# Start of the expert stages of a two-layer decoder trunk: expert 0's rows copied by halves, its gate and up products in PSUM banks 2 and 3, expert 1's first unit and the one-hot turning placed earlier

## The reference, cut to what matters

```python
for i in range(2):                                   # two layers, 512 tokens, 1024 wide
    m = short_conv_mixer(x) if i == 0 else chunked_sgu_mixer(x)
    x = layer_norm(ALPHA * x + m, ln_mix_g[i], ln_mix_b[i])
    # grouped_moe: 16 experts in 4 groups, the best group and two experts in it per token
    scores = sigmoid(x @ router_w); gates = normalised scores of the two chosen
    for e in range(16):
        h = silu(x @ w_gate[e]) * (x @ w_up[e])      # 1024 -> 512
        f = f + gates[:, e] * (h @ w_down[e])        # 512 -> 1024
    x = layer_norm(ALPHA * x + f, ln_ffn_g[i], ln_ffn_b[i])
```

## Time and profile before

| | |
|---|---|
| median of 3 runs | 1126.11 us (1125.99 to 1126.21) |
| profiled execution, its own time | 1129.59 us |
| span of the profiled execution | 1127.8 us |
| PE busy | 1104.9 us (98%) |
| DVE busy | 830.3 us (74%) |
| ACT busy | 652.2 us (58%) |
| POOL busy | 119.1 us (11%) |
| DMA moved | 295.97 MB, mean 262 GB/s |

### The profile page before, as it was taken

How to read it: one execution, slowest core, us unless ns; L and a number is a source line. 1 busy time by engine, 2 the same in 40 slices (tenths; PEclk the granted TensorE clock), 3 DMA queues, 4 the chain that set the end, 5 groups by cost and what they waited for, 6 DMA issues and landing times.

```text
span 1127.8 us, 15394 instructions
## 1 busy us (share of the span) xinstructions
PE 1104.9 (98%) x5448; PEld 871.9 (77%) x5448; DVE 830.3 (74%) x1022; ACT 652.2 (58%) x761; POOL 119.1 (11%) x104
## 2 busy tenths in 40 slices
PE   8999999899999999999999999999999999999996
PEld 7888888577777777778888888888757777777774
DVE  4553547899988999999516555535799798988996
ACT  4322323588887888853417332213558788887872
POOL 2000000031111111030000000000004111111013
PEclk9999999999999999999999999999999999999998
DMA  8925421699999999987304222440399999999986
GB/s 309 418 82 221 149 94 40 227 403 391 393 380 393 371 393 378 399 273 273 149 19 174 88 76 77 156 141 38 121 352 369 395 375 391 377 385 384 383 290 171
DMA packets 51752, 295.97 MB, mean 262 GB/s; under 512 B 8932, under 2 KB 9092, under 8 KB 22128
## 3 DMA queue, kind: packets, MB, share of 16 engines
q1 hardware_dynamic: 36096, 252.46, 58.0%
q0 software_dynamic: 9040, 20.91, 6.4%
q10 hardware_dynamic: 6560, 21.87, 5.1%
HBM read 277.07 MB, written 29.62 MB: 272 GB/s over the span
## 4 chain that ended last, share of the span: by engine, by line
PE 82%; DMA 10%; DVE 3%; issue 2%; ACT 1%; ACTq 0%; SPq 0%; POOL 0%; DVEq 0%; POOLq 0%
PE ps L481 24%; PE ps L483 24%; PE ps L482 24%; DMA raw_more<-in_w_moe 4%; PE ps L2046 2%; DMA raw<-in_w_dense 2%; PE ps L1963 2%; DMA X<-y_rows 1%; PE ps L1888 1%; DVE lo L477 1%; PE ps L2186 1%; PE ps L1870 1%; DMA raw<-in_w_moe 1%; PE ps L1859 1%; PE ps L1988 1%
## 5 line engine op out<-in xcount | busy, mean ns | idle before, releaser
L477 DVE TENSOR_TENSOR lo<-raw,hi 128x1024 fp32r<-128x1024 f32 x320 | 376.5, 1219 | 89.0 <-ACT hi L466 86.5
L466 ACT ACTIVATE hi<-raw 128x1024 fp32r<-128x1024 f32 x320 | 325.0, 1056 | 120.8 <-PE ps L483 80.2
L481 PE MATMUL ps<-hi,xgT_hi 128*112 128x512 f32 x480 | 190.7, 397 | 0.0
L483 PE MATMUL ps<-hi,xgT_lo 128*112 128x512 f32 x480 | 188.6, 393 | 0.0
L482 PE MATMUL ps<-lo,xgT_hi 128*112 128x512 f32 x480 | 187.9, 391 | 0.0
L477 DVE TENSOR_TENSOR lo<-raw_more,hi 128x1024 fp32r<-128x1024 f32 x128 | 153.3, 1220 | 32.9 <-ACT hi L466 30.5
L466 ACT ACTIVATE hi<-raw_more 128x1024 fp32r<-128x1024 f32 x128 | 132.8, 1057 | 56.1 <-DMA raw_more<-in_w_moe 37.1
L481 PE MATMUL ps<-xT_hi,hi 128*128 128x512 f32 x320 | 126.5, 395 | 1.4 <-DVE lo L477 1.4
L482 PE MATMUL ps<-xT_lo,hi 128*128 128x512 f32 x320 | 124.7, 390 | 0.0
L483 PE MATMUL ps<-xT_hi,lo 128*128 128x512 f32 x320 | 124.6, 389 | 0.0
L483 PEld LDWEIGHTS ps<-hi,xgT_lo 128*112 128x112 f32 x480 | 83.7, 174 | 26.5
(11 more groups left out here) (216 smaller groups left out, 1490.0 us busy)
## 6 DMA issues: line engine op xcount, KB each, us to landing
raw<-in_w_moe SPq DMA_DIRECT2D x128, 1024.0 KB, 12.7
raw_more<-in_w_moe SPq DMA_DIRECT2D x64, 1024.0 KB
raw<-in_w_dense SPq DMA_DIRECT2D x39, 1024.0 KB, 5.6
y_rows<-X ACTq DMA_DIRECT2D x4, 2048.0 KB, 25.3
X<-y_rows POOLq DMA_DIRECT2D x10, 512.0 KB, 9.2
x_rows<-X ACTq DMA_DIRECT2D x8, 512.0 KB, 2.6
Y<-y_rows SPq DMA_DIRECT2D x6, 512.0 KB, 5.5
xT_raw<-in_x_t SPq DMA_DIRECT2D x4, 512.0 KB, 6.5
```

The lines of the kernel that those rows point to most:

```text
L466: nc.scalar.activation(hi[:, s, :], flat(raw_units(n)), ACT.Copy).then_inc(hi_ready, 1)
L477: eng.tensor_tensor(lo[:, s, :], flat(raw_units(n)), hi[:, s, :], ALU.subtract).then_inc(lo_ready, 1)
L481: nc.tensor.matmul(out_, a_hi, b_hi, start=first, stop=False)
L483: return nc.tensor.matmul(out_, a_lo, b_hi, start=False, stop=last)
```

## The change

The copies of expert 0's rows are signalled by halves. A new semaphore is raised by product 3 of the last tile, the last that writes bank 5, and ACT's copy waits for it in place of the end of the tile. ACT then waits for the end of the tile before it scales the token tiles, behind a table load. `gate_up_first` starts on ACT's half alone and waits for DVE's half before its product 4.

Expert 0's gate and up go to banks 2 and 3, so that `gate_up(1)` in banks 0 and 1 has no need to wait for `hidden(0)`. Its unit 0 stands directly behind `gate_up_first`, and `turn_h(0)` behind unit 0. `turned_hot` is placed behind unit 6 instead of behind the whole of `gate_up(1)`. On ACT the copy to `hotT` is placed before the `hi` of unit 12 instead of behind `silu(1)`.

The counts move to bank 7, the ids of layer 1 from bank 3 to bank 7. The wait for `most_ready` goes from `turned_hot` to the first `gates_to_slots`, and DVE's `route_most` goes from behind the `lo` of unit 7 to between `x_lo(1)` and `hidden(0)`.

```diff
-        IDA = (7, 3)
+        IDA = 7
+        CNT = 7
@@ ACT, silu
-                    nc.scalar.activation(sgate[0:T, :], ps[0:T, 0, :], ACT.Silu).then_inc(silu_ready, 1)
+                    bank = 2 if is_zero(c) else 0
+                    nc.scalar.activation(sgate[0:T, :], ps[0:T, bank, :], ACT.Silu).then_inc(silu_ready, 1)
@@ ACT, turn(e)
                     for k in range(GU - 1):
+                        if is_zero(e) and k == DN:
+                            act.wait_ge(hotT_in, layer + 1)
+                            copy(hotT[layer][0:T, :, :], ps[0:T, 2:4, :]).then_inc(hotT_ready, 1)
                         if n0 + k not in WHOLE:
                             split_hi(act, n0 + k, step, i)
                     silu(e + 1, step, i)
-                    if is_zero(e):
-                        act.wait_ge(hotT_in, layer + 1)
-                        copy(hotT[layer][0:T, :, :], ps[0:T, 2:4, :]).then_inc(hotT_ready, 1)
@@ ACT, start of the experts
-                act.wait_ge(xgT_ready, m0 + 1)
+                act.wait_ge(x0_half, layer + 1)
                 copy(x0[:, 0:4, 0:T], slots(ps[:, 5:6, :])).then_inc(xgT_hi_ready, 1)
                 preload(ACT.Silu)
+                act.wait_ge(xgT_ready, m0 + 1)
@@ DVE, hidden
-                    nc.vector.tensor_tensor(hid[0:T, :], sgate[0:T, :], ps[0:T, 1, :], ALU.mult).then_inc(hid_ready, 1)
+                    bank = 3 if is_zero(c) else 1
+                    nc.vector.tensor_tensor(hid[0:T, :], sgate[0:T, :], ps[0:T, bank, :], ALU.mult).then_inc(hid_ready, 1)
@@ DVE, start of the experts
                 x_lo(1)
+                route_most(layer)
                 hidden(0)
...
-                route_most(layer)
                 turn(0, gates=True)
@@ PE, first_rows
+                    if t == NT - 1 and k == KD // 2 - 1:
+                        ins.then_inc(x0_half, 1)
@@ PE, gates_to_slots
                 if t == 0:
                     pe.wait_ge(gates_done, layer + 1)
+                    pe.wait_ge(most_ready, layer + 1)
@@ PE, gate_up
-                    if c + m0:
+                    if c != 1:
                         pe.wait_ge(hid_ready, plus(c + m0, i))
@@ PE, turned_hot
-                    pe.wait_ge(most_ready, layer + 1)
@@ PE, gate_up_first
                     pe.wait_ge(xgT_hi_ready, m0 + 1)
-                    pe.wait_ge(xgT_lo_ready, m0 + 1)
...
-                        return nc.tensor.matmul(ps[0:T, h, :], x0[:, k, 0:T], flat(raw_units(n))[:, h * F:(h + 1) * F],
+                        return nc.tensor.matmul(ps[0:T, 2 + h, :], x0[:, k, 0:T], flat(raw_units(n))[:, h * F:(h + 1) * F],
...
                     for k in range(GU - 2):
+                        if k == GU // 2:
+                            pe.wait_ge(xgT_lo_ready, m0 + 1)
@@ PE, experts
+                def beside_first(k):
+                    if k % 2:
+                        gates_to_slots(layer, (k - 1) // 2)
+                    elif k == 0:
+                        turn_h(0)
+                    elif k == GU - 2:
+                        turned_hot()
+
                 gate_up_first()
-                turn_h(0)
-                gate_up(1, between=lambda k: gates_to_slots(layer, (k - 1) // 2) if k % 2 else None)
-                turned_hot()
+                gate_up(1, between=beside_first)
                 turn_x(2)
                 pe.wait_ge(hotT_ready, layer + 1)
                 down(0)
```

More of the change, by code:

```diff
@@ L393, in hybrid_decoder @@
         xg_in = [sem(f"xg_in{b}") for b in range(2)]
+        x0_half = sem("x0_half")
         xgT_ready = sem("xgT_ready")
@@ L1455, in route_ids @@
             def route_ids(layer):
-                es, bank = slice(0, NA), IDA[layer]
+                es, bank = slice(0, NA), IDA
                 dve.wait_ge(ids_ready, layer + 1)
@@ L1465, in route_most @@
                 dve.wait_ge(cnt_ready, layer + 1)
-                chain.step(nc.vector.reduce_max(scr[layer]["most_f"][:, :], ps[:, LGB[layer], 192:192 + E], axis=AX.X))
+                chain.step(nc.vector.reduce_max(scr[layer]["most_f"][:, :], ps[:, CNT, 192:192 + E], axis=AX.X))
                 nc.vector.tensor_copy(most[:, layer:layer + 1], scr[layer]["most_f"][:, :]).then_inc(most_ready, 1)
@@ L1896, in first_ids @@
                 pe.wait_ge(hot_ready, 2 * NT * layer + t + 1)
-                ins = sum_by_slot(hot[layer][t], IDA[layer], t, 0, 3, range(NA))
+                ins = sum_by_slot(hot[layer][t], IDA, t, 0, 3, range(NA))
                 if t == NT - 1:
@@ L1903, in counts @@
                 for u in range(NT):
-                    ins = nc.tensor.matmul(ps[:, LGB[layer], 192:192 + E], ones_b[:, :], sel[:, u, :],
+                    ins = nc.tensor.matmul(ps[:, CNT, 192:192 + E], ones_b[:, :], sel[:, u, :],
                                            start=(u == 0), stop=(u == NT - 1))
```

## The result

The changed kernel takes 1130.24 us (median of 9 runs, 1128.43 to 1133.26), the kernel before 1126.21 on the same chip (9 runs, 1125.99 to 1130.42). The ratio is 1.0033, with a 95% interval of 1.0024 to 1.0042, which is 3.7 us: slower, where I had forecast 1123.6 and given slower 5%. All ratios and intervals leave out disturbed runs, here none, in the experiments one of 3963 us of the kernel before and three of e8 (2255, 5722 and 6366 us). The profiled executions say less than these medians. That of the changed kernel, 1128.43 us, is the fastest of its nine; that of before, 1129.59, is 3.4 us above its median. So the two spans shown differ by -1.0 us while the medians differ by +4.0, and what follows compares stretches, not spans.

A forecast was written before the change was run, and what follows sets the result against it. It took PE, busy 98% of the span, to bound the kernel, with layer 1's end hanging on the weight stream. Gains of 1.35 us in layer 0 and 1.15 in layer 1, 2.5 in all, gave 1123.6, range 1122.0 to 1125.3.

The forecast's parts named there:

- Steps 1 to 4: Expert stage start to unit 12: PE earlier by 1.43 us at the products, 1.5 at unit 1, 1.35 at unit 12.
- Step 5: Unit 12 to layer end: layer 0 keeps 1.35 us; layer 1, hanging on the weight stream, gains 1.15.
- Rival 3: Late pairs for units 24 to 27 leave two stream holes of 3.2 us: 3.6 us slower, 1129.7; 6%.
- Rival 2: Layer 1 is stream-bound and gains only 0.1 us, PE's lead used up waiting: 1124.7; 28%.
- Rival 1: DVE keeps up at unit 12, so PE keeps 1.9 us in both layers: 1122.3; 16%.

The follow-up runs named there:

- e8: Changed kernel with the copy to `hotT` ahead of the `hi` of unit 14 instead of unit 12: 1125.43 us, ratio 0.9988 to the kernel before.
- e2: Changed kernel with `turned_hot` and the copy to `hotT` back in their old places, only the new start kept: 1125.23 us, ratio 0.9991 to the kernel before.
- e3: Kernel before with only `turned_hot` behind unit 6 and the copy ahead of the `hi` of unit 12, old start: 1131.16 us, ratio 1.0044.
- e1: Changed kernel with only the copy to `hotT` put back behind `silu(1)`: 1126.50 us, ratio 1.0000 to the kernel before.
- e5: Kernel before with the 1 MB load of layer norm parameters issued ahead of `x_hi(1)`, before the stream is full: 1125.57 us, ratio 0.9991.
- e6: Kernel before with only the new start, and the 1 MB parameter load issued ahead of `x_hi(1)`: 1122.65 us, ratio 0.9964.

## Why the prediction was wrong

**Steps 1 to 4 were right**, with the layer's own 0.72 us taken off (foreseen in brackets): products 1.49 earlier (1.43), unit 0 1.89 (1.93) behind 0.82 of idle (0.9), unit 1 1.56 (1.5), `down(0)` 2.01 (1.9), unit 12 1.40 (1.35) behind 0.41 of idle (0.55). In layer 1 unit 12 is 1.29 earlier. `first_ids` and `gates_to_slots` had no new wait. Ends of single operations came out within 0.1 us.

**Step 5 failed, in both of its halves.** The first: "nothing else stops PE behind unit 12". I had followed PE and DVE to unit 12 and stopped. The margin of `x_lo` was 1.7 to 3.6 us in layer 0, readable from the trace of before, and where the DMA share is 1.00 for 180 us a stream that is late has no room to catch up. The lead of layer 0, 1.06 us at unit 36 with the 0.72 taken off, was gone by 369 us, and the layer ends 0.69 late. The hole isn't all of it: the smallest margin of before, 1.73, is only 0.33 more than the lead, and e2, with full windows, lost its lead of 1.48 in layer 0 as well.

The second: "the queue is full there (413 GB/s), which hides a late issue". The 413 GB/s are of the window 229 to 247 of the kernel before, in which the late pairs were not late. That the engines are busy doesn't say how much is queued behind the transfer in progress, and this is the step that made the change slower. The count was in the trace of before. From 210 on SyncE has issued 10 pairs (10.49 MB) when the first of the two comes at 239.18, and 11 (11.53 MB) when the second comes at 244.89. Its queue, q1, has by then moved (packets, MB, share of the 16 engines from 210 on):

```profile
q1 hardware_dynamic: 1204, 8.82, 78.5%
...
q1 hardware_dynamic: 1526, 11.19, 82.0%
```

So 1.67 and 0.34 MB were outstanding, and 0.34 MB are 0.9 us at 385 GB/s, less than the 1.25 us by which the second pair was going to be late. In the changed kernel the same count at 239.70 and 245.42 is

```profile
q1 hardware_dynamic: 1348, 9.87, 86.0%
...
q1 hardware_dynamic: 1578, 11.50, 84.2%
```

which leaves 0.62 and 0.03 MB outstanding. The stream had also begun some 1.5 us earlier, which used up the queue sooner: behind its layer's first record the first of these pairs is issued at 43.02 us, against 41.77 before and 40.96 in e2, where the same start has no early copy. Measured so, the pairs came 2.06 us late. The stream of layer 1, for which I had put down a gain of 1.15 us, was 1.3 us behind instead.

**Rival 3 was the right mechanism**, at 6%: hole, place (units 24 to 27) and cause. That its time comes so near (1129.7 against 1130.24) is luck: it had 6.4 us of holes in layer 1 alone and a gain of 1.35 kept in layer 0, while both layers have a hole of about 2.4 to 2.9 us and neither keeps the gain, and it wanted a queue run dry for both pairs, where only the second found it so. The Trainium skill, "DMA: Bandwidth & Descriptors", "Anatomy of one DMA", had given 4.4 us as an estimate for a pair that finds the queue empty; the section is on DMAs that GpSimd issues, while these come from SyncE. The second late pair of layer 0 was issued at 245.42, and by count its last packet came 4.6 us later, so the trace agrees within 0.3 us there; in layer 1 it took 5.5, nearer to the 5.7 of the earlier trace rows, which I had put in. By the 4.4 us two holes would be 3.8 us, nearer to what was seen in one layer than 6.4, yet the total by it, 1127.2, is too low, because layer 0's lead was counted as kept.

Rival 2 came true for what it says, that PE's lead is used up waiting, but in both layers, not in one, and not for its time, 1124.7. Rival 1 did not: PE did wait at unit 12.

The account by ratios: the early turning and copy on the old start +5.0 us (e3), on the new start +4.7 (e2 to the changed kernel); the new start -1.0 (e2) of 3.0. With the parameter load out of the way the start is worth 2.9 and the copy's place costs 1.5, so some 3.2 of its 4.7 us are paid because the stream has no room. The two effects don't add; each is as large as the stream's margin lets it be.

Open is why e1, without a hole, gains nothing, how much of the 3.7 us is the hole and how much the missing room, and what sends some executions of the kernel before into a layer 1 that is held from expert 4 on and others not. That e5 has no such executions (11 runs within 1.7 us) speaks for the stream's margin as the switch; nothing shows what throws it.

## What to carry to other kernels

A full transfer window is no reserve: before delaying an instruction that frees a buffer, count the bytes that are outstanding at that moment. Where they last for less time than the delay, the rest is a hole, and if the stream is needed at its full rate afterwards, reckon with losing it. For each lead that PE is to gain, find the operand that arrives last in every later period (here `x_lo`) and read how long it has been ready; the smallest such margin caps the gain. And look for transfers that aren't urgent inside the full stretch: 1 MB moved ahead of it was worth 1.0 us to the kernel before, 3.0 to the earlier start (e2 to e6) and 5.7 to the changed kernel, by the ratios.

## What the runs showed of the hardware

- PE's 512-column matmuls are spaced in one of two ways at a granted clock of 1.00. The 48 of a `gate_up` take 10.83 or 10.84 us from the first start to the last for every expert from 2 on in e5 and e6 and in layer 0 of the kernel before, and 11.05 for expert 10 of layer 0 in the changed kernel: 0.229 against 0.233 us for one, 2%. The slower spacing is also that of `down(0)` in all four kernels, whether PE waited ahead of it (0.34 us before) or not (changed kernel), and most experts that `x_lo` holds do not have it (6 to 9 of layer 0 in the changed kernel: 10.85 to 10.87). So being held isn't the reason by itself; what is, isn't settled.
- How long a 1 MB pair takes depends on what is queued ahead of it. The second late pair of the changed kernel, with 0.03 MB ahead of it in layer 0 and 0.06 in layer 1, had its last packet 4.6 and 5.5 us after its issue. The four pairs for `raw` that the kernel before issues from 259 to 280, with the parameter load beside them, land after 12.6 us in the median.
- In windows of 6 us the DMA share is 1.00 to 1.02 at rates from 339 to 425 GB/s: rate alone doesn't show that the engines have room. For holes the share is the column to read.
